# A hybrid decoder step on one core: V pages in two buffers, a weight ring of four until the FFN, the order of the loads, and the first K pages loaded and turned early

## The reference

```python
h = rmsnorm(x, norm1_g);  z = h @ w_in            # 2048 -> 4096: q, k, v (8 heads x 128), u (1024)
# sample tokens: 16 pages of 128 cached keys per sequence, found through page_table
k_mean = mean of each block of 256 keys           # 8 blocks
idx    = top_k(q . k_mean, 3)                     # per head and query
s      = q . k * D**-0.5 - slope * distance       # only keys of the chosen blocks, and the new ones
a      = softmax(s) @ v
# prompt tokens: causal attention within the 256 tokens, same slopes
p      = (windowed mean of u - u) @ w_pool * pool_scale
x      = x + concat(a, p) @ w_out
x      = x + (silu(h2 @ w_gate) * (h2 @ w_up)) @ w_down     # h2 = rmsnorm(x, norm2_g), 5632 wide
y      = rmsnorm(x, norm_f_g)
```

## Time and profile before

| | us |
|---|---|
| median of 3 runs | 1667.96 (1659.04 to 1668.64) |
| the profiled execution | 1665.54 |
| its span | 1663.6 |
| up to the first logits | 95.6 |
| attention loop, iteration 0 | 53.6 |
| iterations 1 to 5 together | 327.6 |
| iterations 6 and 7 | 61.8 and 63.6 |
| tail, to the end of the pooling half of w_out | 136.2 |
| the rest (w_out, FFN, final norm) | 925.4 |
| mean granted clock of TensorE | 0.94 of 2.4 GHz |

### The profile page before, as it was taken

The page is one execution under the profiler, slowest core; times in us unless marked ns, Lnnn a source line. Parts: engine busy times, 40 slices in busy tenths (PEclk is TensorE's granted clock), DMA queues, the critical chain, the costliest instruction groups (busy, mean ns, idle before and its releaser), DMA issues.

```text
span 1663.6 us, 34175 instructions
## 1 busy us (share of the span) xinstructions
PE 1458.1 (88%) x13918; PEld 1333.7 (80%) x13918; DVE 888.3 (53%) x1319; ACT 502.9 (30%) x666; POOL 105.1 (6%) x184
## 2 busy tenths in 40 slices
PE   6968877788863557899999999999999999999987
PEld 5957556566641235799999999999999999999986
DVE  4566556465563424456645555554545455465545
ACT  4311111121110023335543433333333334343333
POOL 2007220000000010002000000000000000000003
PEclk9988899989986777999999999999999999999998
DMA  6647988988977663655555555555555555555541
GB/s 204 209 160 257 351 305 290 347 330 302 338 278 271 242 189 92 203 181 165 165 165 165 164 164 164 164 164 164 164 164 164 164 165 164 164 164 165 165 138 69
DMA packets 162343, 334.40 MB, mean 201 GB/s; under 512 B 10207, under 2 KB 52248, under 8 KB 161663
## 3 DMA queue, kind: packets, MB, share of 16 engines
q1 hardware_dynamic: 162247, 333.06, 60.7%
HBM read 328.10 MB, written 5.27 MB: 200 GB/s over the span
## 4 chain that ended last, share of the span: by engine, by line
PE 75%; DMA 10%; SPq 6%; DVE 5%; issue 3%; ACT 1%; POOL 0%; POOLq 0%; ACTq 0%; DVEq 0%
PE banks L1222 22%; PE banks L1224 21%; PE banks L1223 21%; DMA vpage<-in_cache_v 6%; PE banks L1316 4%; DMA w_raw<-in_w_in 3%; SPq L385 3%; PE banks L1333 3%; PE banks L1228 2%; SPq L406 2%; SPq L394 1%; DVE kpage L808 1%; DVE w_lo L724 1%; ACT w_hi L502 1%; DMA vec<-in_pool_scale 1%
## 5 line engine op out<-in xcount | busy, mean ns | idle before, releaser
L724 DVE TENSOR_TENSOR w_lo<-w_raw,w_hi 128x1024 fp32r<-128x1024 f32 x360 | 440.2, 1230 | 540.8 <-ACT w_hi L502 539.8
L1222 PE MATMUL banks<-hh,w_hi 128*128 128x288 f32 x2176 | 659.8, 303 | 42.4 <-DVE w_lo L724 35.3
L1223 PE MATMUL banks<-hl,w_hi 128*128 128x288 f32 x2176 | 652.4, 300 | 0.0
L1224 PE MATMUL banks<-hh,w_lo 128*128 128x288 f32 x2176 | 650.1, 299 | 0.0
L502 ACT ACTIVATE w_hi<-w_raw 128x1024 fp32r<-128x1024 f32 x360 | 378.7, 1058 | 747.3 <-PE banks L1224 508.7
L1222 PEld LDWEIGHTS banks<-hh,w_hi 128*128 128x128 f32 x2176 | 418.1, 192 | 66.7 <-DVE w_lo L724 39.7
L1224 PEld LDWEIGHTS banks<-hh,w_lo 128*128 128x128 f32 x2176 | 420.0, 193 | 0.0
L1223 PEld LDWEIGHTS banks<-hl,w_hi 128*128 128x128 f32 x2176 | 419.1, 193 | 0.1
L1222 PE MATMUL banks<-ah,w_hi 128*128 128x288 f32 x704 | 210.0, 298 | 9.5 <-DVE af L1078 5.4
L1224 PE MATMUL banks<-ah,w_lo 128*128 128x288 f32 x704 | 210.2, 299 | 0.0
L1223 PE MATMUL banks<-al,w_hi 128*128 128x288 f32 x704 | 206.9, 294 | 0.0
(11 more groups left out here) (182 smaller groups left out, 681.5 us busy)
## 6 DMA issues: line engine op xcount, KB each, us to landing
kpage<-in_cache_k SPq DMA_DIRECT2D x128, 512.0 KB, 5.6
vpage<-in_cache_v SPq DMA_DIRECT2D x128, 512.0 KB, 5.9
w_raw<-in_w_gate SPq DMA_DIRECT2D x88, 512.0 KB, 3.6
w_raw<-in_w_up SPq DMA_DIRECT2D x88, 512.0 KB, 3.6
w_raw<-in_w_down SPq DMA_DIRECT2D x88, 512.0 KB, 3.7
w_raw<-in_w_in SPq DMA_DIRECT2D x64, 512.0 KB, 8.4
w_raw<-in_w_out SPq DMA_DIRECT2D x32, 512.0 KB, 4.1
xs<-in_x_prompt SPq DMA_DIRECT2D x2, 1024.0 KB, 8.1
```

Source lines behind the costliest of these rows:

```text
L724: V.tensor_tensor(w_lo[:, s, :], w_raw[:, s, :], w_hi[:, u, :].bitcast(F32), ALU.subtract).then_inc(lo_ready, 1)
L1222: PE.matmul(o, wh, xh[:, c, :], start=start and i == 0, stop=False)
L1223: PE.matmul(o, wh, xl[:, c, :], start=False, stop=False)
L1224: last = PE.matmul(o, wl, xh[:, c, :], start=False, stop=stop and i == len(chunks) - 1)
```

## The change

It does six things. (a) `w_raw` has 4 slots until the FFN and 6 from there on; the memory of the two late slots lies under `z` until then (`tile_at`, `slot_free`). (b) `vpage` has two buffers with a semaphore each. (c) SP's order in the loop, for unit n, becomes: K of unit n+2, tiles 2n+4 and 2n+5, V of unit n-2. (d) The page table is loaded at the start, and the eight pages of the first two K units are loaded between the q tiles 6 to 13; VectorE turns the first unit before the last q tile is waited for. (e) VectorE turns unit (i+1,0) at the very end of iteration i, after `take_block` and `osb_high(i-1)`; TensorE issues block_sums(i-1) ahead of logits(i,0), and both tiles of the first quarter ahead of joint_max(i-1). (f) The table `rel` is not loaded at the start but after the last logits, into memory that is free by then; after the loop SP issues `rel`, `w_pool` and four w_out tiles behind the V pages of unit 29, and then the V pages of units 30 and 31.

```diff
-RAW = 6
+RAW = 4
+RAW_FF = 6
@@
+    if k < T_FF:
+        return k, k // RAW, k % RAW, k % HI
+    m = k - T_FF
+    s = m % RAW_FF
+    earlier = T_FF // RAW if s < RAW else 0
+    return k + per * i, earlier + m // RAW_FF + (per // RAW_FF) * i, s, k % HI
+
+def slot_free(t):
+    n, _, s, _ = t
+    if isinstance(n, int) and n < T_FF + RAW_FF:
+        if n < T_FF + RAW:
+            return n - RAW + 1
+        return T_OA + 1
+    return n - RAW_FF + 1
@@
-        vpage = sb("vpage", [P, 4, AW], stack=kv)
+        vpage = sb("vpage", [P, 2, 4, AW], stack=kv)
@@ SP
+            def load_v(n):
+                if n >= 2:
+                    sp.wait_ge(v_done, n - 1)
+                elif n == 0:
+                    sp.wait_ge(xT_in, KC)
+                    sp.wait_ge(hist_T, 2)
+                for g in range(4):
+                    sp.dma_start(vpage[:, n % 2, g, :], page(cv, n // NQUADS, 4 * (n % NQUADS) + g)
+                                 ).then_inc(v_in[n % 2], 16)
@@
                 load(tile_at(T_Q + k), w_in_d[256 * j:256 * j + 256, 512 * c:512 * c + 512], free=k >= RAW)
+                if k == 6:
+                    sp.wait_ge(pages_in, 16)
+                if 6 <= k < 14:
+                    load_k_page((k - 6) // 4, (k - 6) % 4)
+            for k in range(4):
+                load_kvu(k)
+            for n in range(NQUADS * NB):
+                if n + 2 < NQUADS * NB:
+                    load_k(n + 2)
+                for k in (2 * n + 4, 2 * n + 5):
+                    if k < 8 * KVU_STEPS:
+                        load_kvu(k)
                 if n >= 2:
+                    load_v(n - 2)
             sp.wait_ge(qk_done, NQUADS * NB)
+            sp.dma_start(rel[:, :], A["tables"][:, a:b]).then_inc(rel_in, 16)
             sp.dma_start(wpool[:, :, :, :], ...)
-            load_v(NB - 1, 0)
             load_out_pool(range(4))
-            load_v(NB - 1, 1)
-            load_out_pool(range(4, 8))
-            load_v(NB - 1, 2)
-            load_out_pool(range(8, 10))
-            load_v(NB - 1, 3)
-            load_out_pool(range(10, 12))
+            load_v(NQUADS * NB - 2)
+            load_v(NQUADS * NB - 1)
+            load_out_pool(range(4, 12))
@@ VectorE
             for k in range(6, 16):
                 if k < 12:
                     lo(tile_at(4 + k))
+                if k == 12:
+                    turn_k(0, 0)
@@
             pad_q(0)
-            turn_k(0, 0)
@@
                 if i < NB - 1:
                     scaled_logits(i)
                     pad_q(i + 1)
-                    turn_k(i + 1, 0)
                 if i < KVU_STEPS:
                     take_block(2 * i + 1)
                 if i:
                     osb_high(i - 1)
+                if i < NB - 1:
+                    turn_k(i + 1, 0)
@@ TensorE
-                logits(i, 0)
                 if i:
                     block_sums(i - 1)
+                logits(i, 0)
                 if i >= 2:
                     combine(i - 2)
                 if i < KVU_STEPS:
                     kvu_tile(8 * i)
+                    kvu_tile(8 * i + 1)
                 if i:
                     joint_max(i - 1)
-                if i < KVU_STEPS:
-                    kvu_tile(8 * i + 1)
-                if i:
                     p_turned(i - 1)
```

More of the change, by code:

```diff
@@ L153, in sb @@
             return (stack or ctx).enter_context(nc.sbuf_tensor(name, shape, dt))
-        tab = sb("tab", [P, A["tables"].shape[1]])
+        tab = sb("tab", [P, at["rel"][0]])
         xT = sb("xT", [P, KC, T])
@@ L170, in step_program @@
         nrm = sb("nrm", [P, 2, T])
+        raw = ExitStack()
+        w_raw = sb("w_raw", [P, RAW_FF, TE], stack=raw)
+        raw.close()
+        raw = ExitStack()
+        w_lo = sb("w_lo", [P, RAW_FF, TE], F32R, stack=raw)
+        raw.close()
+        sb("w_mid", [P, RAW, TE])
         mid = ExitStack()
@@ L223, in step_program @@
         ktok = sb("ktok", [P, 2, AW], stack=post)
+        rel = sb("rel", [P, 384], stack=post)
         px = sb("px", [P, 2, 384], stack=post)
@@ L243, in step_program @@
         late = ExitStack()
+        sb("w_more", [P, RAW_FF - RAW, TE], stack=late)
         sg = sb("sg", [P, 4, T], stack=late)
@@ L355, in _ @@
             xp, xsam = A["x_prompt"][0], A["x_sample"].rearrange("b q d -> (b q) d")
-            sp.dma_start(tab[:, :], A["tables"]).then_inc(tab_in, 16)
+            sp.dma_start(tab[:, :], A["tables"][:, 0:at["rel"][0]]).then_inc(tab_in, 16)
             for n in range(2):
@@ L371, in load, with page, load_k_page, load_k @@
                              src.rearrange("(k p) n -> p k n", p=P)).then_inc(w_in_s[s], 16)
+            sp.dma_start(pages[:, :], A["page_table"].rearrange("b n -> (b n)").rearrange("(a n) -> a n", a=1)
+                         ).then_inc(pages_in, 16)
+            def page(pool, b, n):
+                e = NPAGES * b + n
+                idx = sp.value_load(pages[0:1, bass.ds(e, 1)], min_val=0, max_val=pool.shape[0] - 1)
+                return pool[bass.ds(idx, 1), :, :].rearrange("a t n -> (a t) n")
+            def load_k_page(n, g):
+                sp.dma_start(kpage[:, n % 2, g, :], page(ck, n // NQUADS, 4 * (n % NQUADS) + g)
+                             ).then_inc(k_in[n % 2][g], 16)
+            def load_k(n):
+                sp.wait_ge(qk_done, n - 1)
+                for g in range(4):
+                    load_k_page(n, g)
+            def load_v(n):
[4 more added lines that the diff above has]
+                    sp.wait_ge(hist_T, 2)
+                for g in range(4):
+                    sp.dma_start(vpage[:, n % 2, g, :], page(cv, n // NQUADS, 4 * (n % NQUADS) + g)
+                                 ).then_inc(v_in[n % 2], 16)
+            def load_kvu(n):
+                m, r = n // 4, n % 4
+                c0 = 4 * AW - CW * (m + 1)
+                load(tile_at(T_KVU + n), w_in_d[512 * r:512 * r + 512, c0:c0 + CW])
             for k in range(16):
@@ L755, in x_taken, with turn_k @@
                 V.tensor_copy(xT[:, c, :], XB[c % 3][:, 0:T]).then_inc(x_ready, 1)
+            def turn_k(i, j):
+                n = NQUADS * i + j
+                for g in range(4):
+                    dve.wait_ge(k_in[n % 2][g], 16 * (n // 2) + 16)
+                    V.transpose(kpage[:, n % 2, g, :], kpage[:, n % 2, g, :]).then_inc(k_turned, 1)
             for c in range(X_AHEAD):
@@ L976, in _ @@
                     dve.wait_ge(a_out, s + 1)
-                    own.link(V.scalar_tensor_tensor(px[:, s % 2, :], tb("rel"), 2.0 ** -(s + 1), px[:, s % 2, :],
+                    if s == 0:
+                        dve.wait_ge(rel_in, 16)
+                    own.link(V.scalar_tensor_tensor(px[:, s % 2, :], rel[:, :], 2.0 ** -(s + 1), px[:, s % 2, :],
                                                     ALU.mult, ALU.add))
@@ L1314, in values @@
                 for x in range(2):
-                    for n in range(4):
-                        last = PE.matmul(OB[x][32 * n:32 * n + 32, :], pT[:, n, bass.ds(j, 32, 4)],
-                                         vpage[:, n, 512 * x:512 * x + 512], start=j == 0, stop=j == NQUADS - 1)
+                    for g in range(4):
+                        last = PE.matmul(OB[x][32 * g:32 * g + 32, :], pT[:, g, bass.ds(j, 32, 4)],
+                                         vpage[:, n % 2, g, 512 * x:512 * x + 512], start=j == 0,
+                                         stop=j == NQUADS - 1)
                 last.then_inc(v_done, 1)
```

62 lines of the change are left out of this document (9 added, 53 removed).

## The result

| | before | after |
|---|---|---|
| median (lowest to highest), us | 1668.30 (1659.04 to 1670.91), 4 runs | 1598.76 (1595.69 to 1600.51), 4 runs |
| the profiled execution, us | 1665.54 | 1595.69 |
| its span, us | 1663.6 | 1593.9 |

The ratio is 0.959, 95% interval 0.955 to 0.963. The change makes the kernel 69.5 us faster; the forecast was 1607, range 1582 to 1640. In the 16 runs of `before` taken beside the experiments the median is 1665.8 us (1654.9 to 1670.7), by which the gain is 67 us. The profiled execution of `after` is the fastest of its four.

The account below looks back on a forecast made before the run. In iterations 1 to 5 TensorE's chain, with waits chiefly for V pages, and the DMA engines compete as bounds, neither full. Terms sum to -60.0: 1665.5 becomes 1605.5 profiled, the median 2.4 higher; forecast 1607 us, range 1582 to 1640.

Parts of the forecast that it names:

- The bound, and what frees it: Attention loop: TensorE waits mostly for late V pages; issuing V two units before use removes V and weight waits, 12 us an iteration.
- rival 1: Attention loop: DMA engines bring more than 367 GB/s and pauses cost no clock; about 1585 us, chance 0.14.
- Rival 2: Attention loop: the DMA queue is the bound at 340 GB/s, no gain in iterations 1 to 5; about 1632 us, chance 0.15.
- rival 4: Iterations 0 to 5: weight tiles land late in the ring of four, making the kernel slower; about 1690 us, chance 0.04.
- Rival 3: Attention loop: waits only change names, V in time but K later by as much; about 1656 us, chance 0.05.
- The start: Before the first logits: the first unit's four turns leave the chain, -4.5 us, of which 0 to 2 could come back.
- Iteration 0: First attention iteration: four weight tiles are there when the loop starts, 53.6 us becomes 44.6, -9.0 us.
- Iterations 1 to 5: Attention loop: 61.1 us an iteration with two new pauses, over a DMA floor of 57.5; -22 us, between -37 and -5.
- The clock: Iterations 1 to 5: each of TensorE's two pauses costs 1.5 us of slow clock, between 0 and 2.5.
- Iterations 6 and 7: Last two attention iterations: TensorE waits for K issued behind V; 125.3 us becomes 96.3, -29.0 us, between -20 and -35.
- The tail: After the attention loop: `w_pool`, w_out tiles 4 and 5 and the stores come later; +4.5 us, between 1 and 9.
- The rest: After the tail: TensorE is busy without a gap, so the stretch stays as long as before, 0 us.

Follow-up runs that it names:

- the table of four kernels: `after` with two V buffers or one (V loads also placed differently), part (e) kept or undone: two 1598.8 and 1560.5 us, one 1701.0 and 1635.0.
- The kernel with the new placement alone: `before` with only w_raw and w_lo, still six slots, placed in memory behind six small buffers: 1655.9 us, ratio 0.994.
- K first: `after` with K of unit n+3 issued ahead of V of unit n-2 in SP's program: 1594.3 us, ratio 0.956.
- The edit of the tail's loads: `after` with `rel` and `w_pool` issued ahead of V of unit 28, and w_out tiles 4 and 5 ahead of V of unit 31: 1584.9 us, ratio 0.951.

## Why the prediction was right, and where its steps were not

**The bound, and what frees it: right.** V pages were the wait, and the second buffer with its loads removes it: 75 or 102 us by the table of four kernels, and 112.2 us of waits for V come back without it. Of rival 1 the first half is true (more than 367 GB/s can be had) and the second is not (the pauses did cost clock). Rival 2 falls with the 390 GB/s of the kernel without part (e), rival 4 with the 5.1 us of weight waits in all. Rival 3 has a grain in it: the waits did change their name to K, but 78.2 us (73.1 for K, 5.1 for weights) stand for what were 143.6 (91.4 for V, 35.3 for weights, 16.9 for K), and about 50 of the 73.1 are the pauses of part (e), not a late K.

**The start (-4.5, measured -7.7).** The turns left the chain with 4.3 us, between the end of the q stage and the first logits. The other 3.3 us fell before that end (83.03 before, 79.69 now). The kernel with the new placement alone ends its q stage at 80.09, so nearly all of this part comes without the rest of the change. Up to 1.4 us of it is TensorE's wait for the first load (13.68 us before, 12.24 now), which differs as much among kernels that start alike. No step of the prediction had this part.

**Iteration 0 (-9.0, measured -9.7): right.** Four tiles are there when the loop starts.

**Iterations 1 to 5 (-22, measured -26.3): right for its own sum, with a false bound beside it.** The two pauses came as worked out: 5.35 us where I had 5.3, and 23.6 us to logits(i,1) where I had 22.2. An iteration took 60.3, forecast 61.1. The step that failed is "a full share would be 367 GB/s, so 57.5 us. That is the other bound for iterations 1 to 5". Dividing GB/s by the share assumed that a share of 1 is the end and that share and bytes go together up to it. The runs showed 390 to 394 GB/s at a share of 1.03 to 1.04, held for 265 us, and iterations of 53.0 us. The row of 399 GB/s had said so, and I took it for a burst. The forecast was spared because the pauses kept the kernel above either floor. But I also took from it that "at most 7.8 can be had" of the 16 us; 12.5 an iteration were there (65.5 to 53.0), and part (e) gave away 7.2 of them (60.3 for 53.0). At the full pace GB/s over share is 378 or 379, so the short cut was wrong in both its parts: the quotient was low, and the share does not end at 1.

**The clock.** I took 1.5 us for each pause, 3 an iteration. In iteration 3 the unit behind the first pause took 4.53 us and the one behind the second 4.06, for 2.76: 1.8 and 1.3 us, 3.1 together. In iterations 1 to 5 the units in both places took 4.04 to 4.53 us, and the mean is again 3.1 an iteration. Undoing part (e) raised the clock of these iterations from 0.91 to 0.98. The prediction also named what the Trainium skill (TensorE: Matmul & The Clock Gate, Part 1, What's actually happening) says, that the slow state is the default and activity releases it. With the whole unit at the slow level behind each pause, 4.52 for 2.76 us, the price is 3.5 us an iteration. That is 0.5 more than mine, not the 3 more that the prediction wrote. The rows lie between: some units pay the full price and some less.

**Iterations 6 and 7 (-29, measured -34.6).** The mechanism was right: TensorE waits 11.53 and 10.09 us for the K that stands behind V. That K did not come sooner than forecast: from SP's issue of V to logits(6,3) are 15.3 us (452.64 to 467.95), where the forecast has 14.4. The mis-sized term is the two values units at the end. I put them at the slow clock, 6.8 us for the pair; they took 4.07 in iteration 6 and 3.67 in iteration 7, which is 5.9 us together and the whole of the difference. "K first" moved the wait on to V. It won nothing in these iterations beside part (e), and about 6 us with part (e) undone.

**The tail (+4.5, measured +12.1): the term that was mis-sized most.** `w_pool` had been put at 2.3 us and took 6.56. The two last values units before the loop's end run back to back and at full clock, so SP began V(28) only 0.9 us before the end, not 3.4. The eight V pages then took 8.96 us to issue, and `w_pool` was issued 8.5 us after the end. I had read 0.9 us a page out of 3.63 us for four, but the starts lie 1.1 us apart. The w_out tiles 4 and 5 had been put at 1.7 and the wait there rose by 4.0 (2.50 to 6.52): issued from 601.78 on, they landed 7.4 and 8.7 us later, not the 5 to 7 that I gave them. The edit of the tail's loads recovers 14 us by the medians and 12.1 by the traces, so this order is all of the loss. My "between 1 and 9" did not hold it.

**The rest (0, measured -3.5).** No part of the prediction looked at where the buffers lie. The diff moved `w_raw`, and this gives some 10 us of the 70 with the piece at the start. Without it my sum of -60 would have been just about met, but by luck: a tail too cheap by 7.6 us stood against attention iterations too dear by 10. Two sums of the prediction are off by a little as well: 1605.5 and 2.4 make 1608, not 1607, and the terms of rival 2 make about 1635, not 1632.

**What the change is made of, by the runs.** The second V buffer with its loads carries it; part (e) costs 38 us, the order of the tail's loads 12 to 14; the placement gives 10, early K 2 to 5, and K behind V costs 6 to 7 once part (e) is undone. What the new order of K, tiles and V gives by itself, with two buffers, was not measured. Without the three costly orders the same buffers run in 1540.1 us, 7.7% under before.

## What to carry to other kernels

When an edit bundles a buffer with new orders, price the orders separately: here the buffer with its loads was worth 75 to 102 us and the three orders beside it cost 58.7. Before work is queued behind a wait on an in-order engine, write out what stands behind that wait and who is waiting for it; here both the turns behind `osb_high` and the turns behind `joint_max` stopped TensorE, and the stops took the clock as well. And do not read a ceiling of the DMA engines off a stretch in which they idle part of the time; the fullest stretch of the trace, even a short one, is nearer to it.

## What the runs showed of the hardware

- The DMA engines of one core sustained 390 to 394 GB/s, the lower figure over 265 us, in a mix of K and V pages and weight tiles, and the share reads up to 1.04 there. GB/s over share pointed at 367 where the share was 0.87 or 0.88.
- The same matmuls at the same granted clock ran 0.7% faster (260 weight tiles in 823.8 us for 829.6) when the weight buffers lay behind some small buffers rather than ahead of them, and the whole kernel 0.6%. Why is open.
- Behind pauses of some 5 us, in which TensorE had almost nothing to do, a logits unit took 4.04 to 4.53 us, for 2.76 at full clock.
- Page loads whose address SP takes from the page table start 1.1 us apart in SP's queue (eight in 8.8 to 9.0 us); two weight loads took 0.98 us together.
